# One hybrid decoder layer with 16 experts on one core: results combined in float32r, gate and up weights in whole 2 MB units, the tenth unit and the last one in halves

## The reference, cut to what matters

```python
hg = jnp.einsum('nd,edf->nef', xt, w_gate)      # 16 experts, d = 2048, f = 512
hu = jnp.einsum('nd,edf->nef', xt, w_up)
a = jax.nn.silu(hg) * hu * combine[:, :, None]
out = jnp.einsum('nef,efd->nd', a, w_down)
x = layer_norm(ALPHA * x + out, ln2_g, ln2_b)
```

## Time and profile before

| | us |
|---|---|
| median of 3 runs | 891.53 (889.98 to 893.04) |
| the profiled execution, its own time | 890.04 |
| its span from first to last instruction | 888.1 |
| TensorE busy | 842.9 (95%) |
| VectorE busy | 285.5 (32%) |
| ScalarE busy | 264.6 (30%) |
| granted TensorE clock, mean | 0.987 |
| weights and other data moved | 267.84 MB |

### The profile page before, as it was taken

The page is one execution under the profiler, slowest core; times in us unless marked ns, Lnnn a source line. Parts: engine busy times, 40 slices in busy tenths (PEclk is TensorE's granted clock), DMA queues, the critical chain, the costliest instruction groups (busy, mean ns, idle before and its releaser), DMA issues.

```text
span 888.1 us, 11130 instructions
## 1 busy us (share of the span) xinstructions
PE 842.9 (95%) x4734; PEld 558.0 (63%) x4734; DVE 285.5 (32%) x387; ACT 264.6 (30%) x471; POOL 21.2 (2%) x37
## 2 busy tenths in 40 slices
PE   5999999999999999998999999999999998898993
PEld 5989999999999999996433333433333333333331
DVE  5374474433764544426001002133003120031203
ACT  5234232322233232313423322432223321222101
POOL 0000000000001000000000000010000100000000
PEclk9999999999999999998999999999999999999997
DMA  9655553565544885587998999999999999999980
GB/s 291 197 144 128 190 166 127 192 201 161 155 143 146 285 286 185 158 321 275 375 423 352 427 420 424 426 422 422 424 425 418 423 427 422 421 424 423 425 357 34
DMA packets 91135, 267.84 MB, mean 302 GB/s; under 512 B 13850, under 2 KB 68944, under 8 KB 69641
## 3 DMA queue, kind: packets, MB, share of 16 engines
q1 hardware_dynamic: 85930, 258.45, 75.8%
q0 software_dynamic: 1920, 5.30, 1.5%
q10 hardware_dynamic: 3238, 3.43, 1.2%
HBM read 263.07 MB, written 11.54 MB: 309 GB/s over the span
## 4 chain that ended last, share of the span: by engine, by line
PE 70%; DMA 18%; DVE 6%; ACT 3%; SPq 2%; issue 1%; POOL 0%; POOLq 0%; ACTq 0%; DVEq 0%
PE ps L1327 16%; PE ps L501 12%; PE ps L503 12%; PE ps L502 12%; DMA gu_w<-in_expert_w_up 7%; PE ps L1361 6%; DMA down_w<-in_expert_w_down 4%; PE ps L1263 3%; DMA out<-xg,sample_row 3%; DMA xg<-z_rows,row 2%; SPq L403 2%; DMA raw<-in_w_in 1%; ACT xT L1436 1%; PE ps L1207 1%; DVE xg L1684 1%
## 5 line engine op out<-in xcount | busy, mean ns | idle before, releaser
L1327 PE MATMUL ps<-gu_w,xT 128*64 128x512 f32 x1024 | 235.0, 601 | 12.6 <-DMA gu_w<-in_expert_w_up 11.8
L1327 PEld LDWEIGHTS ps<-gu_w,xT 128*64 128x64 f32 x1024 | 72.6, 137 | 140.0 <-issue 136.0
L501 PE MATMUL ps<-xT_hi,w_hi 128*128 128x320 f32 x512 | 159.2, 311 | 0.0
L709 DVE TENSOR_TENSOR w_lo<-raw,w_hi 128x2048 fp32r<-128x2048 f32 x50 | 114.5, 2290 | 137.0 <-ACT w_hi L701 134.8
L503 PE MATMUL ps<-xT_hi,w_lo 128*128 128x320 f32 x512 | 158.2, 309 | 0.0
L502 PE MATMUL ps<-xT_lo,w_hi 128*128 128x320 f32 x512 | 158.2, 309 | 0.0
L701 ACT ACTIVATE w_hi<-raw 128x2048 fp32r<-128x2048 f32 x49 | 93.8, 1915 | 207.6 <-DMA raw<-in_w_in 137.8
L1436 ACT ACTIVATE xT<-ps,gbT 128x64 f32<-128x64 f32 x256 | 82.2, 406 | 153.5 <-PE ps L1263 153.5
L1361 PE MATMUL ps<-down_w,aT 128*64 128x512 f32 x480 | 106.5, 596 | 0.6
L1706 DVE TENSOR_TENSOR a_sb<-ps,a_sb 128x256 f32<-128x256 f32 x16 | 6.8, 424 | 289.1 <-ACT a_sb L1491 289.1
L501 PEld LDWEIGHTS ps<-xT_hi,w_hi 128*128 128x128 f32 x512 | 96.1, 188 | 0.5
(11 more groups left out here) (267 smaller groups left out, 554.8 us busy)
## 6 DMA issues: line engine op xcount, KB each, us to landing
gu_w<-in_expert_w_gate SPq DMA_DIRECT2D x64, 1024.0 KB, 13.4
gu_w<-in_expert_w_up SPq DMA_DIRECT2D x64, 1024.0 KB, 15.8
down_w<-in_expert_w_down SPq DMA_DIRECT2D x32, 2048.0 KB, 23.3
raw<-in_w_in SPq DMA_DIRECT2D x34, 1024.0 KB, 5.4
raw<-in_w_out SPq DMA_DIRECT2D x16, 1024.0 KB, 5.3
tok<-in_x_prompt SPq DMA_DIRECT2D x2, 1024.0 KB, 6.3
z_rows<-z_part ACTq DMA_DIRECT2D x8, 256.0 KB, 6.0
tok<-in_x_sample SPq DMA_DIRECT2D x1, 512.0 KB, 9.8
```

Of the source, the lines that this page charges most:

```text
L501: pe.matmul(out, wh[:, t, col], hi[:, kt, :], start=(n == 0 and t == 0), stop=False)
L709: dve.tensor_tensor(w_lo[k][:, :], raw[k][:, :], w_hi[k][:, :].bitcast(FP32), ALU.subtract)\
L1327: last = pe.matmul(ps[C * side:C * (side + 1), GU, :], x, w[:, :, c, FH * side:FH * (side + 1)], start=(j == 0 and c == 0), stop=(j == PAI ...
```

## The change

- **Gate/up units.** From expert 1 on, a unit is the gate or the up weights of half the features (16 KB runs, from expert 2 on in one DMA of 2 MB; expert 1's first unit was issued in the mixer and keeps two DMAs, its others have one). `gate_up(e, j)` for e >= 1 takes its gate columns from the even unit and its up columns from the odd unit of a pair: at j = 0 and j = 2 it waits for both, and `ring_used` goes up by 2 behind j = 1 and j = 3. Expert 0 is read as before. The gate product stands on partitions 0 to 63 and the up product on 64 to 127, each 512 columns wide, so that silu and its multiplication are 64 x 512 instead of 128 x 256, and `turn_a` has four transposes instead of two.
- **xT** has one buffer instead of two.
- **Combining.** `gatedT` becomes `placeT`, ones and zeros in float32r, and `gate_of_slot` the gate value of each result row; both are made by VectorE from the bank that ScalarE used to copy. ScalarE writes gate times result, rounded, to `y_hi`; VectorE writes the remainder to `y_lo` and then counts `y_ready`. `combine` has eight float32r matmuls instead of four in float32.
- **Unit 9**, (0,5): its first MB is issued at once, its second behind `group0_ready`.
- **The last unit**, (15,5): two DMAs of 1 MB. `down` takes the first half's products for both column halves of the output, then waits for the second half. `half_down` is counted at three quarters of the unit instead of half.
- Small tiles are moved in memory.

```diff
-    DMAS = [2 if u < PAIRS else 1 for e, u in ORDER]
+    SPLIT = EARLY + 4
+    LAST = len(ORDER) - 1
+    DMAS = [2 if i == SPLIT or u < PAIRS and (e == 0 or (e, u) == (1, 0)) else 1 for i, (e, u) in enumerate(ORDER)]
...
         src = (gate_v, up_v)[n]
+        if e:
+            src, c = gate_v, 4 * n
...
-            elif i == EARLY + 4:
-                sp.wait_ge(group0_ready, 1)
             if i >= FIRST:
                 sp.wait_ge(ring_used, units_used(i))
+            if i in (SPLIT, LAST):
+                for n in range(2):
+                    if i == SPLIT and n:
+                        sp.wait_ge(group0_ready, 1)
+                    sp.dma_start(down_w[s][:, n, :], down_v[:, e, u - PAIRS, n, :])\
+                      .then_inc(last_in if i == LAST and n else unit_full[s], 16)
+                continue
             if u < PAIRS:
-                for n in range(2):
-                    load_half(sp, i, n)
+                sp.dma_start(gu_w[s][:, :, :].rearrange("p g c -> p (g c)"),
+                             (gate_v, up_v)[u % 2][:, e, u // 2, :, :].rearrange("p c f -> p (c f)"))\
+                  .then_inc(unit_full[s], 16)
...
-                for h in range(2):
-                    half = slice(C * h, C * (h + 1))
-                    last = pe.matmul(ps[:, ACC + 2 * h + q, :], gatedT[half, k, :],
-                                     y[half, 512 * q:512 * (q + 1)], start=(k == 0), stop=(k == EG - 1))
+                for n, y in enumerate(parts):
+                    for h in range(2):
+                        half = slice(C * h, C * (h + 1))
+                        last = pe.matmul(ps[:, ACC + 2 * h + q, :], placeT[half, k, :],
+                                         y[half, 512 * q:512 * (q + 1)], start=(k == 0 and n == 0),
+                                         stop=(k == EG - 1 and n == 1))
...
+            if e == 0:
+                i = AT[e, j]
+                pe.wait_ge(unit_full[slot(i)], all_in(i))
+                sides = [gu_w[slot(i)][:, side, :].rearrange("p (c f) -> p c f", c=4) for side in range(2)]
+                used = 1
+            else:
+                at_half = [AT[e, j // 2 * 2 + side] for side in range(2)]
+                if j % 2 == 0:
+                    for i in at_half:
+                        pe.wait_ge(unit_full[slot(i)], all_in(i))
+                sides = [gu_w[slot(i)][:, j % 2, :].rearrange("p (c f) -> p c f", c=4) for i in at_half]
+                used = 2 * (j % 2)
             for c in range(4):
-                x = xT[e % 2][:, j, c, :]
+                x = xT[:, j, c, :]
                 for side in range(2):
-                    last = pe.matmul(ps[C * side:C * (side + 1), GU, :], x,
-                                     w[:, :, c, FH * side:FH * (side + 1)],
+                    last = pe.matmul(ps[C * side:C * (side + 1), GU, :], x, sides[side][:, c, :],
                                      start=(j == 0 and c == 0), stop=(j == PAIRS - 1 and c == 3))
-            last.then_inc(ring_used, 1)
+            if used:
+                last.then_inc(ring_used, used)
...
             for c in range(FT // 2):
-                last = pe.transpose(ps[:, bank, P * c:P * (c + 1)], a_sb[:, c:FH:2], ident[:, :])
+                for h in range(2):
+                    last = pe.transpose(ps[:, bank, P * c + C * h:P * c + C * (h + 1)],
+                                        a_sb[:, FH * h + c:FH * (h + 1):2], ident[0:C, 0:C])
...
+                for k in range(4):
+                    n, q = (k // 2, k % 2) if i == LAST else (k % 2, k // 2)
+                    f = 2 * u + n
+                    if i == LAST and k == 2:
+                        pe.wait_ge(last_in, 16)
...
+        def high(to, src, g, k):
+
+            act.activation(to, src, ACT.Copy, scale=gate_of_slot[:, g, k:k + 1]).then_inc(y_hi_ready, 1)
...
-                act.copy(y_sb[:, :].rearrange("p (b c) -> p b c", b=2), ps[:, Y:Y + 2, :]).then_inc(y_ready, 1)
+                act.wait_ge(gatedT_ready, g + 1)
+                high(y_hi[:, :].rearrange("p (b c) -> p b c", b=2), ps[:, Y:Y + 2, :], g, k)
...
-            act.activation(a_sb[:, :], ps[:, GU, 0:FH], ACT.Silu).then_inc(silu_ready, 1)
+            act.activation(a_sb[:, :], ps[0:C, GU, :], ACT.Silu).then_inc(silu_ready, 1)
...
+        def turned_places(g):
+
+            dve.wait_ge(gatedT_full, g + 1)
+            steps.inc(dve.tensor_reduce(gate_of_slot[:, g, :], ps[:, MS, :].rearrange("p (k s) -> p k s", k=EG), AXX,
+                                        ALU.add))
+            dve.wait_ge(dve_step, steps.value)
+            dve.tensor_scalar(placeT[:, :, :].rearrange("p k s -> p (k s)"), ps[:, MS, :], 0.0, None,
+                              ALU.not_equal).then_inc(gatedT_ready, 1)
+
+        def low(e, to, src, high):
+
+            g, k = where(e)
+            dve.scalar_tensor_tensor(out=to, in0=src, scalar=gate_of_slot[:, g, k:k + 1], in1=high.bitcast(FP32),
+                                     op0=ALU.mult, op1=ALU.subtract).then_inc(y_ready, 1)
...
-            dve.tensor_tensor(a_sb[:, :], ps[:, GU, FH:F], a_sb[:, :], ALU.mult).then_inc(a_ready, 1)
+            dve.tensor_tensor(a_sb[:, :], ps[C:2 * C, GU, :], a_sb[:, :], ALU.mult).then_inc(a_ready, 1)
+            if k == 1:
+                turned_places(g)
             if k == 1 and g:
                 finish(g - 1)
...
+            if e:
+                dve.wait_ge(y_hi_ready, e)
+                low(e - 1, y_lo[:, :], ps[:, Y:Y + 2, :].rearrange("p b c -> p (b c)"), y_hi[:, :])
+        for q, bank in enumerate((GU, MS)):
+            col = slice(512 * q, 512 * (q + 1))
+            dve.wait_ge(y_hi_ready, NE + q)
+            low(NE - 1, last_lo[:, col], ps[:, bank, :], last_hi[:, col])
         finish(NG - 1)
```

More of the change, by code:

```diff
@@ L221, in hybrid_trunk_kernel @@
     LG = NG + 1
+    FACTS = 3 + 2 * EG
     logits = little("logits", [P, 3, NR])
@@ L242, in hybrid_trunk_kernel @@
     esum = little("esum", [P, 3])
+    rest = little("rest", [P, 3, NE])
+    ahead = little("ahead", [P, 3, NE])
+    small[0] = max(small[0], MISC + 3 * KB)
+    facts = little("facts", [P, 3, NG, FACTS])
+    group_rank = little("group_rank", [P, 3, NG])
+    token_i = little("token_i", [P, 3], INT32)
+    token = little("token", [P, 3])
+    number = little("number", [P, 4], F32R)
     gbT = little("gbT", [P, 2, 2, HK])
@@ L253, in hybrid_trunk_kernel @@
     spare = little("spare", [P, 1])
-    rest = little("rest", [P, 3, NE])
-    ahead = little("ahead", [P, 3, NE])
     row_no = little("row_no", [P, 1])
     fits = little("fits", [P, 1])
-    gates_of = little("gates_of", [P, 3, NE])
     one_of = little("one_of", [16, 16], F32R)
@@ L266, in hybrid_trunk_kernel @@
     unit_full = [S(f"unit_full{s}") for s in range(FIRST)]
-    ring_used = S("ring_used")
+    ring_used, last_in = S("ring_used"), S("last_in")
     hi_ready, lo_ready = S("hi_ready"), S("lo_ready")
@@ L1355, in down @@
                 pe.wait_ge(unit_full[slot(i)], all_in(i))
-                for q in range(2):
-                    for n in range(2):
-                        f = 2 * u + n
-                        for side in range(2):
-                            col = HD * side + 512 * q
-                            last = pe.matmul(ps[C * side:C * (side + 1), out + q, :], turned[:, f % 2, f // 2, :],
-                                             down_w[slot(i)][:, n, col:col + 512],
-                                             start=(f == 0), stop=(f == FT - 1))
-                    if e == NE - 1 and u and q == 0:
+                for k in range(4):
[3 more added lines that the diff above has]
+                        pe.wait_ge(last_in, 16)
+                    for side in range(2):
+                        col = HD * side + 512 * q
+                        last = pe.matmul(ps[C * side:C * (side + 1), out + q, :], turned[:, f % 2, f // 2, :],
+                                         down_w[slot(i)][:, n, col:col + 512],
+                                         start=(f == 0), stop=(f == FT - 1))
+                    if i == LAST and n and q == 0:
                         last.then_inc(half_down, 1)
@@ L1457, in results @@
                 act.wait_ge(half_down, 1)
[L1458 removed]
+                high(last_hi[:, 0:512], ps[:, GU, :], g, k)
             act.wait_ge(ring_used, AT[e, UNITS - 1] + 1)
             if e == NE - 1:
[L1461 removed]
+                high(last_hi[:, 512:HD], ps[:, MS, :], g, k)
             else:
[L1463 removed]
+                act.wait_ge(gatedT_ready, g + 1)
+                high(y_hi[:, :].rearrange("p (b c) -> p b c", b=2), ps[:, Y:Y + 2, :], g, k)
         def root(g):
```

50 lines of the change are left out of this document (21 added, 29 removed).

## The result

The kernel after takes **901.62 us**, the median of 4 runs (898.92 to 909.26), against 890.75 for the kernel before in the same comparison (4 runs, 888.55 to 893.04). The ratio is 1.0133, 95% interval 1.0099 to 1.0167. A second comparison gave 900.77 (6 runs, 897.92 to 910.35) against 890.21, ratio 1.0120 [1.0092, 1.0148]. So the change costs 10.6 to 10.9 us. I had forecast +3.5, with a range that ended at 899.5. The direction was right, the size was not.

A forecast was written before the change was run, and what follows sets the result against it. The end was taken to hang on the last weight units' landing, then TensorE's work. Terms -0.6 (landing of (15,3)) + 2.8 + 0.3 + 1.0 gave +3.5 us: 895.0 us, range 888.5 to 899.5.

The forecast's parts named there:

- What bounds it: Whole kernel: the end hangs on the last units' landing, then TensorE's work; before 484 us TensorE's pace places the stream.
- Head start of unit 9: Unit 9's first MB, moved ahead of `group0_ready`: 2.5 us of lead, lost in later gaps; taken as 0.
- Gathers late: Rival, much slower: first gather delayed by unit 9's first MB, experts start 1 to 2.4 us late; 899.5 us, chance 0.15.
- Longer runs: Gate/up weight stream: 16 KB packets save 10 ns per 16 KB, -3.9 us over 48 units from (4,0) to (15,3).
- Release in pairs: Weight stream near 485 us: (2,5) waits and goes out with (4,0), which lands +2.1; with later odd units +3.3 us.
- TensorE per expert: Each expert: transposes and silu add 0.5 us on TensorE; cost 0, covered by 2.8 us an expert.
- The last expert: Expert 15: two quarters remain behind the last gate/up landing; the last down matmul's end moves by +2.8 us.
- Behind the last matmul: Kernel's end: both remainders come before VectorE's statistics, which end 3.9 us after the last matmul against 3.6; +0.3 us.
- Rows gathered amid the stream: Experts 7 and 11: scatters up to 5.5 us longer beside 16 KB packets, TensorE loses about 6 us each; taken +1.0.
- The stream keeps its lead: Rival, faster: gaps at 474 and 484 us do not reset the weight stream; -3.9 us, 887.6 us, chance 0.2.
- Nothing moves: Rival, same: release in pairs costs 1.4 us and the gathers nothing; +0.6 us, 892.1 us, chance 0.3.
- The rounded combine is no faster: Rival: float32r row pairs don't overlap, combine(14) stays at 1.9 us; +1.0, 896.0 us, no chance given.

The follow-up runs named there:

- the pair without write-out: Kernel before, and kernel after with unit 9 whole behind `group0_ready`, both without the scatters of groups 0 to 2: 883.55 and 889.07 us.
- the control: Kernel before without the scatters of groups 0 to 2 (those output rows left out): 883.55 us, ratio 0.9922.
- the kernel without the early half: Kernel after with both halves of unit 9 issued behind `group0_ready`: 898.00 us, ratio 1.0078; again 898.45 us, ratio 1.0090.

## Why the prediction was wrong, by its own steps

First the profiled executions, term by term, forecast against measured:

| | forecast | measured |
|---|---|---|
| (4,0) lands | +2.1 | +4.0 |
| from there to the landing of (15,3) | -2.7 | +0.8 |
| TensorE's start behind that landing | +1.0 | +1.1 |
| last expert, to the last down matmul's end | +2.8 | +2.5 |
| behind it | +0.3 | +0.4 |
| sum | +3.5 | +8.8 |

**What bounds it.** Right for before. The view that the end hangs on the landing of the last units is what broke: in the kernel after TensorE set the end. In none of the four traces of it, with or without the early half, does TensorE wait for a landing from 600 us on. The prediction had named this as the sign of being wrong.

**Head start of unit 9.** Taken 0, and 0 was right for the gain. Its price for the first gather was left out of the sum and stood only in the rival "Gathers late", at 1 to 2.4 us; TensorE waited 0 to 6.6 us for it in the five traces, and the runs show 2.3 to 3.6 us at the median. The rows I used for it come from an execution with nothing of the stream beside the store, so 2.3 us of slack was no guide to the size.

**Longer runs.** Packets: with 16 KB alone, 765 to 785 us,

```profile
DMA packets 590, 8.57 MB, mean 428 GB/s; under 512 B 67, under 2 KB 67, under 8 KB 67
...
q1 hardware_dynamic: 589, 8.55, 100.6%
```

523 large packets in 1.006 x 16 x 20 = 322 us of engine time: 615 ns, forecast 617. The rate rose from 424 to 428 GB/s. The Trainium skill, "DMA: Bandwidth & Descriptors", section Specifications, has 512 B as the least transfer for full rate; here 16 KB still gave 1% over 8 KB. In the pair without write-out the stretch from (4,0)'s landing to (15,3)'s shrank by 2.4 us (494.1 to 841.8 against 499.0 to 844.3), and forecast was -3.9 + 1.2 = -2.7. The term was right in this one pair. In the kernel after it was lost to TensorE's stalls: with nothing released, the stream ran short (365 GB/s above), and (15,3) came +4.8.

**Release in pairs.** (2,5) at 485.1 and 7.7 us to landing, forecast; 485.8 and 8.0, measured. (4,0) at 497.7, forecast; 499.6: 0.7 from the later start of the experts, the rest mostly because (4,0) landed 5.8 us behind (2,5) and not 4.9. Alone in the kernel before the step cost 2.9 us, forecast 3.3.

**TensorE per expert.** +0.5, forecast; +0.57 in each ordinary expert. "Cost 0, cover 2.8 us an expert" is **the first step that failed**. The cover exists only where the stream sets the pace. Ahead of 484 us it does not, there TensorE's lateness places the stream. The partitions by themselves cost 4.5 us, with the rounded combine 2.6. And from expert 7 on the cover had to pay for two stalls, 7.0 + 1.8 and 6.0 + 1.9 us. TensorE is 15.7 us behind the kernel before at the start of expert 11 and 5.9 at the start of the last landing's quarter, so cover there was, but not enough.

**The last expert.** From gate_up(15,2) to the last down matmul's end 26.97 us, forecast 27.3. combine(14) costs 1.13 instead of 1.92. **Behind the last matmul**: +0.4, forecast +0.3. Both right.

**Rows gathered amid the stream** is **the term that was mis-sized** in the profiled execution. The mechanism was right: a scatter longer by 4 to 5 us (bound 5.5), about 6 us lost at expert 7 and again at 11 (7.0 and 6.0), TensorE 1.6 us behind its pair at the end (1.3). What I took for it, +1.0, counted only that last lateness. It left out that a stalled TensorE also stops releasing places, so that the stream falls back, and that the clock is low afterwards: the stretch from (4,0) to (15,3) missed its forecast by 3.5 us, so the term is 4.6 with the 1.1 at the end. In medians its size stays open: 2.3 us by the control, give or take 2.8, and taking the 16 KB runs back bought 1.4 net, while it gave up the stream's own gain, 3.9 by the forecast's estimate.

**The sum again**, in medians: 5.8 for the units without any scatter (forecast 2.5), 2.3 for the late rows beyond before's own (1.0), 2.3 to 3.6 for the early half (0): 10.4 to 11.7, measured 10.6 to 10.9. That the sum closes proves nothing: the parts are differences of the same few runs, and the first two add up to the kernel without the early half by construction. Of the 3.3 us missed in the first, the traces place nearly all ahead of (4,0), where the kernel without write-out is 4.9 us behind its counterpart; 1.5 us of that is a difference in (4,0)'s landing between two executions of before's order at the same issue time (495.6 and 494.1), which I can't explain.

**The rivals.** "The stream keeps its lead" needed (2,5) at about 480: it went at 485.8. "Nothing moves" priced the gathers at nothing. "Gathers late" had the mechanisms, at 15%, and was still 2 us short. "The rounded combine is no faster" is refuted: 1.13 against 1.92 us.

## What to carry to other kernels

Before making a stream's packets longer, look at which small or indirect transfers share its engines and how much slack their users have: here the stream gained 1% (424 to 428 GB/s), and a scatter beside it took 15.4 to 16.0 us instead of 11.1 to 11.2. Slack given as "us per step" must be spent only once, and only where that resource is really the one waited for; add up every lateness that draws on it. And when an experiment takes something out, run the same removal on the kernel before: here the control took 6.9 of the 9.2 us away, and what is left is not clear of the noise. When parts are added up to a whole, ask whether they were measured or follow from each other.

## What the runs showed of the hardware that I had not expected

- A wait of TensorE of 2 us is at times enough for the lower clock afterwards, and at times not: of eleven traces with the new partitions expert 1 took 27.1 us in five (the kernel after among them), 28.6 to 28.8 in five and 30.1 in one, though the wait of 2.0 us at the first `weights_back` stands in those of both sorts. In the six traces with the old partitions, where the wait is 1.8 us, it was 26.5 each time. After 6.4 to 7.0 us of waiting at expert 7 the next quarter was slow each time: 5.43, 5.63 and 5.96 us instead of 3.65. Shorter waits there did it too: 5.31 us after 4.7, and 6.10 after 2.9.
- The indirect gather of group 0 landed 5.7 to 6.8 us after its issue where the stream started 1.4 us or more behind it, and 12.8 and 12.9 us after where it started 0.3 us behind.
- 1 MB of weights, issued ahead of the rows' store, widened the spread of the whole kernel's time with the new units from 3 to 12 us (six runs each) and from 6 to 10 us (four runs each).
